# Hybrid diffusion step on one core: the norm modulation of two tiles on ScalarE and GpSimd, and layer 1 adaLN units taken at other places

## The reference, cut to what matters

```python
def _modulate(x, shift, scale):
    return _layernorm(x) * (1 + scale) + shift

for i in range(DEPTH):
    sh_a, sc_a, g_a, sh_f, sc_f, g_f = _ada(c, w_ada[i], b_ada[i])
    h = _modulate(x, sh_a, sc_a)
    out = attention(h) if i % 2 == 0 else _fourier_mix(h, w_fourier_out[0])
    x = _post_norm(x, g_a * out, ln_gain[i, 0], ln_bias[i, 0])
    h = _modulate(x, sh_f, sc_f)
    moe = _hier_moe(h, ...)
    x = _post_norm(x, g_f * moe, ln_gain[i, 1], ln_bias[i, 1])
```

## Time and profile before

| | us |
|---|---|
| median of 3 runs | 1063.76 (1063.31 to 1065.43) |
| profiled execution, own time | 1065.38 |
| its span, first to last instruction | 1063.6 |
| TensorE busy | 835.2 (79%) |
| VectorE busy | 329.9 (31%) |
| ScalarE busy | 166.0 (16%) |
| GpSimd busy | 158.7 (15%) |
| DMA | 318.11 MB, 299 GB/s mean |

### The profile page before, as it was taken

How to read it: one execution, slowest core, us unless ns; L and a number is a source line. 1 busy time by engine, 2 the same in 40 slices (tenths; PEclk the granted TensorE clock), 3 DMA queues, 4 the chain that set the end, 5 groups by cost and what they waited for, 6 DMA issues and landing times.

```text
span 1063.6 us, 13809 instructions
## 1 busy us (share of the span) xinstructions
PE 835.2 (79%) x4921; PEld 442.9 (42%) x4922; DVE 329.9 (31%) x803; ACT 166.0 (16%) x354; POOL 158.7 (15%) x245
## 2 busy tenths in 40 slices
PE   3899999969987888988778855997589877787740
PEld 3556565635466333323323334664533322332310
DVE  2113555544754111111111128247411110111117
ACT  0122222233010111111111112110111111101110
POOL 1032030311111120211101101101111111101010
...
GB/s 336 367 350 91 220 176 130 80 367 82 235 328 248 165 417 260 420 421 420 419 412 407 347 309 375 204 252 178 227 217 421 420 420 419 419 417 413 368 127 79
DMA packets 90242, 318.11 MB, mean 299 GB/s; under 512 B 13150, under 2 KB 26174, under 8 KB 65624
## 3 DMA queue, kind: packets, MB, share of 16 engines
...
## 4 chain that ended last, share of the span: by engine, by line
PE 50%; DMA 35%; DVE 6%; issue 4%; SPq 2%; ACT 2%; POOL 1%; ACTq 0%; DVEq 0%; POOLq 0%
DMA ring<-in_w_expert_up 24%; PE psum L916 15%; PE psum L799 8%; DMA ring<-in_w_ada 6%; PE psum L745 6%; PE psum L938 4%; PE psum L694 4%; PE psum L771 3%; DMA arena<-h_scratch,gidx 2%; DMA y_scratch<-arena,sidx 2%; PE psum L903 1%; DMA arena<-y_scratch 1%; SPq L366 1%; PE psum L1091 1%; PE psum L850 1%
## 5 line engine op out<-in xcount | busy, mean ns | idle before, releaser
L916 PE MATMUL psum<-ring,arena 128*64 128x512 f32 x1088 | 260.0, 633 | 60.6 <-DMA ring<-in_w_expert_up 56.6
L916 PEld LDWEIGHTS psum<-ring,arena 128*64 128x64 f32 x1088 | 93.4, 146 | 223.2 <-issue 221.1
L938 PE MATMUL psum<-ring,arena 128*64 128x512 f32 x544 | 125.9, 604 | 30.9 <-DVE arena L1666 29.6
L1662 DVE TENSOR_TENSOR arena<-arena,psum 128x256 f32<-128x256 f32 x34 | 14.3, 421 | 309.6 <-ACT arena L1215 309.6
L799 PE MATMUL psum<-ring,hT 128*128 128x384 f32 x288 | 98.2, 495 | 0.0
L938 PEld LDWEIGHTS psum<-ring,arena 128*64 128x64 f32 x544 | 40.2, 138 | 93.2 <-issue 77.8
L694 PE MATMUL psum<-ring,silu 128*32 128x128 f32 x1536 | 55.8, 305 | 27.4 <-DMA ring<-in_w_ada 26.9
L576 POOL DMA_INDIRECT y_scratch<-arena,sidx x34 | 34.4, 1012 | 250.9 <-DVE arena L1672 250.9
L745 PE MATMUL psum<-ring,hT 128*128 128x512 f32 x160 | 70.2, 595 | 1.1 <-ACT hT L1288 0.7
L799 PEld LDWEIGHTS psum<-ring,hT 128*128 128x128 f32 x288 | 54.5, 194 | 35.0 <-issue 1.5
L1672 DVE COPY arena<-psum 128x512 f32<-128x512 f32 x34 | 23.5, 692 | 134.4 <-PE psum L938 134.4
...
## 6 DMA issues: line engine op xcount, KB each, us to landing
...
```

Of the source, the lines that this page charges most:

```text
L916: last = pe.matmul(bank[b][64 * e:64 * e + 64, :].rearrange("p (g n) -> p g n", g=2), mem.GT[b][:, c, 64 * e:64 * e + 64], w, start=(c == ...
L938: last = pe.matmul(bank[5 + half][64 * e:64 * e + 64, :], mem.actT[b][:, f, 64 * e:64 * e + 64], w[:, f, 512 * half:512 * half + 512], sta ...
```

## The change

The modulation of tiles 0 and 1 leaves VectorE. VectorE makes statistics, the negated mean and variance; GpSimd makes the root and the product -mean * rstd (`normbias`); ScalarE makes x * rstd + normbias over 1024 columns; GpSimd multiplies by the scale row and adds the shift row, each in two halves of 512. Tile 2 stays on VectorE. Rows for prompt and sample have a buffer each; the sample's are loaded right after the gates in layer 0, and after the prompt's shift and the position matmuls in layer 1. Layer 1's unit 1 is made in attention stage 4 beside unit 0; unit 2 follows the prompt tile's turn, unit 3 the first two routers, units 4 and 5 the last router, and none is left behind the tables. The weight pieces alternate between regions, and expert 1 is loaded after unit 3, experts 2 and 3 after unit 5. In GpSimd's queue the first head root goes ahead of `store_m`. In stage 4 `project_head` goes ahead of the value product. The projections of both sample tiles run before any turn. Semaphore declarations and the wait of `head_transposes` for 13 units at head 7 are left out below.

```diff
@@ -50,16 +50,16 @@
-BETWEEN = {1: [(0, 4), (0, 5), (0, 6)], 2: [(0, 7), (0, 8), (0, 9)], 3: [(0, 10), (0, 11)], 4: [(1, 0)]}
-SPOTS = {3: (1, 3, 5), 2: (1, 4), 1: (4,)}
-PLACES = {"Q0": 0, "Q1": 24, "A0": 48, "A1": 64, "A2": 80, "B0": 0, "B1": 16, "B2": 32}
+BETWEEN = {1: [(0, 4), (0, 5), (0, 6)], 2: [(0, 7), (0, 8), (0, 9)], 3: [(0, 10), (0, 11)], 4: [(1, 0), (1, 1)]}
+SPOTS = {1: (1, 3, 5), 2: (1, 3, 5), 3: (1, 4), 4: (1, 4)}
+PLACES = {"Q0": 0, "Q1": 24, "A0": 48, "A1": 64, "A2": 80, "C1": 24, "B0": 0, "B1": 16, "B2": 32}
-PLACE.update({("ada", 1, u): "A2" for u in range(6)})
+PLACE.update({("ada", 1, u): place for u, place in enumerate(("A2", "C1", "A2", "C1", "A0", "A1"))})
...
@@ -140,6 +140,8 @@
         self.rstd = sb("rstd", [P, TILES])
+        self.negmean = sb("negmean", [P, TILES])
+        self.normbias = sb("normbias", [P, TILES])
         self.mx = sb("mx", [P, 2, 2])
@@ -214,7 +216,8 @@
         self.G = [view(0, D), view(4, D), view(46, D)]
-        self.lnshift = view(46, D)
+        self.lnscale = [self.lnscale_p[:, :], view(12, D)]
+        self.lnshift = [view(46, D), view(26, D)]
         self.wr_group = view(46, 2 * KC * GROUPS).rearrange("p (l n) -> p l n", l=2)
...
@@ -339,15 +344,22 @@
-                at = [(4, 0), (1, 1), (1, 2), (1, 3), (7, 0), (6, 0), (2, 0), (7, 0), (3, 0), (2, 0), (7, 0), (2, 0)][u]
+                at = [(4, 0), (4, 0), (1, 1), (1, 2), (1, 3), (7, 0), (2, 0), (7, 0), (3, 0), (2, 0), (7, 0), (2, 0)][u]
-        ADA_AFTER = {(0, 1): (0, 2), (0, 3): (0, 1), (1, 9): (1, 6), (1, 10): (1, 7), (1, 11): (1, 9)}
+        ADA_AFTER = {(0, 1): (0, 2), (0, 3): (0, 1), (1, 1): (1, 0), (1, 9): (1, 6), (1, 10): (1, 7), (1, 11): (1, 9)}
+
+        def wait_expert_row(eng, l, t):
+
+            if t < TILES - 1:
+                eng.wait_ge(mod_ready, 2 * l + t + 1)
+            else:
+                eng.wait_ge(last_ready, l + 1)
@@ -419,19 +431,21 @@
             load("ada", 1, 0)
-            for e in range(2):
-                sp.wait_ge(qkv_ps, 18 + 6 * e)
-                load_expert(0, e)
-            for u in range(1, 4):
-                after_ada(1, u - 1)
+            sp.wait_ge(qkv_ps, 18)
+            load_expert(0, 0)
+            sp.wait_ge(qkv_ps, 24)
+            load("ada", 1, 1)
+            for u in (2, 3):
+                after_ada(1, u - 2)
                 load("ada", 1, u)
             sp.wait_ge(proj_ps, 6)
-            load_expert(0, 2)
             for u in (4, 5):
-                after_ada(1, u - 1)
                 load("ada", 1, u)
+            after_ada(1, 3)
+            load_expert(0, 1)
             after_ada(1, 5)
-            load_expert(0, 3)
+            for e in (2, 3):
+                load_expert(0, e)
             for l in range(2):
@@ -594,33 +608,61 @@
 
+            HALVES = [slice(0, 512), slice(512, D)]
+
+            def scale(l, t):
+
+                i, n = (0 if t == 0 else 1), 2 * l + t + 1
+                pool.wait_ge(root_out, roots[0])
+                pool.tensor_tensor(mem.normbias[:, t:t + 1], mem.negmean[:, t:t + 1], mem.rstd[:, t:t + 1], ALU.mult
+                                   ).then_inc(bias_out, 1)
+                pool.wait_ge(rows_in_for[i], 32 * (l + 1))
+                pool.wait_ge(centred, n)
+                for part in HALVES:
+                    last = pool.tensor_tensor(mem.tmp[:, t, part], mem.tmp[:, t, part], mem.lnscale[i][:, part], ALU.mult)
+                link(last)
+
+            def shift(l, t):
+
+                i = 0 if t == 0 else 1
+                for part in HALVES:
+                    last = pool.tensor_tensor(mem.h[:, t, part], mem.tmp[:, t, part], mem.lnshift[i][:, part], ALU.add)
+                last.then_inc(mod_ready, 1)
+
             def norm_rows(l, i):
-                spread(mem.lnscale[:, :], l, 4, i, lnscale_in)
-                spread(mem.lnshift, l, 3, i, lnshift_in)
-
+                spread(mem.lnscale[i], l, 4, i, rows_in_for[i])
+                spread(mem.lnshift[i], l, 3, i, rows_in_for[i])
+
+            head_root()
             store_m(0, 4, ADA_UNITS, ADA_AT[0, 11])
             pool.wait_ge(router_ready, 4)
             norm_rows(0, 0)
-            for _ in range(3):
+            for _ in range(2):
                 head_root()
...
                 spread(mem.gates[:, i, :], 0, 2, i, gates_in[i])
+            norm_rows(0, 1)
 
...
                 if l == 1:
-                    pool.wait_ge(norm_ready, 9)
+                    pool.wait_ge(norm_ready, 6)
                     spread(mem.gates[:, 1, :], 1, 2, 1, gates_in[1])
...
                 for t in range(TILES):
-                    for _ in range(2):
-                        root([t])
-                    if t == 0:
-                        pool.wait_ge(norm_ready, 6 * l + 4)
-                        norm_rows(l, 1)
+                    root([t])
+                    if t >= 1 + l:
+                        shift(l, t - 1)
+                    root([t])
+                    if t < TILES - 1:
+                        scale(l, t)
+                    if t == 0 and l == 1:
+                        shift(l, t)
+                        pool.wait_ge(four_ps, KC + 2)
+                        norm_rows(1, 1)
                 if l == 1:
@@ -674,7 +716,7 @@
                     if l == 0 and tiles == [0]:
-                        pool.wait_ge(norm_ready, 7)
+                        pool.wait_ge(norm_ready, 4)
                         spread(mem.gates[:, 0, :], 1, 2, 0, gates_in[0])
...
@@ -864,7 +906,7 @@
             for u in range(1, 5):
-                spots = SPOTS[len(BETWEEN[u])]
+                spots = SPOTS[u]
                 for s in range(6):
@@ -878,12 +920,12 @@
                         ada(*BETWEEN[u][spots.index(s)])
+                    if u == 4 and s >= 1:
+                        project_head(s - 1)
                     if g >= 1:
...
                         turn_head(s)
-                        if s >= 1:
-                            project_head(s - 1)
             pd_transposes(STEPS - 1)
@@ -974,34 +1016,30 @@
 
-                project(l, 1, (2, 3), (0,))
-                if l == 0:
-                    pe.wait_ge(proj_used, 2)
-                    ada(1, 1)
-                project(l, 1, (2, 3), (1,))
-                project(l, 2, (6, 7), (0,))
-                pe.wait_ge(norm_ready, 6 * l + 4)
+                project(l, 1, (2, 3))
+                project(l, 2, (6, 7))
+                wait_expert_row(pe, l, 0)
+                pe.wait_ge(proj_used, 6 * l + 2)
                 turn(0, (4, 5), strided=True)
                 if l == 0:
                     ada(1, 2)
-                project(l, 2, (6, 7), (1,))
-                if l == 0:
-                    ada(1, 3)
-                pe.wait_ge(norm_ready, 6 * l + 5)
+                wait_expert_row(pe, l, 1)
                 wait_turn(pe, TURN_ROUTE[l], 0)
...
                     pe.wait_ge(router_ready, 4)
-                pe.wait_ge(proj_used, 6 * l + 2)
                 router(l, 0)
                 wait_turn(pe, TURN_ROUTE[l], 1)
                 router(l, 1)
-                pe.wait_ge(norm_ready, 6 * l + 6)
+                if l == 0:
+                    ada(1, 3)
+                wait_expert_row(pe, l, 2)
                 turn(2, (4, 5), strided=True)
...
                     ada(1, 4)
+                    ada(1, 5)
                     pe.wait_ge(tables_in, 16)
@@ -1025,8 +1063,6 @@
                     last.then_inc(table_ps, 1)
-                if l == 0:
-                    ada(1, 5)
 
@@ -1036,7 +1072,7 @@
             def turn_tile(t):
-                pe.wait_ge(norm_ready, 7 + t)
+                pe.wait_ge(norm_ready, 4 + t)
                 turn(t, TURN_BANKS[t])
@@ -1225,7 +1261,11 @@
                 for t in range(TILES):
-                    act.wait_ge(norm_ready, 6 * l + 4 + t)
+                    if t < TILES - 1:
+                        act.wait_ge(bias_out, 2 * l + t + 1)
+                        nc.scalar.activation(mem.tmp[:, t, :], mem.x[:, t, :], ACT.Identity, bias=mem.normbias[:, t:t + 1],
+                                             scale=mem.rstd[:, t:t + 1]).then_inc(centred, 1)
+                    wait_expert_row(act, l, t)
                     act.dma_start(h_dram[l].rearrange("(k t p) n -> t p k n", k=2, p=P)[t],
@@ -1544,14 +1584,19 @@
                         dve.wait_ge(gb_used, 2 * l + 1)
+                    if t < TILES - 1:
+                        link(tile_stats(t))
+                        link(V.bn_aggr(mem.mv[:, t, :], mem.stats[:, t, :, :].rearrange("p i n -> p (i n)")))
+                        V.tensor_scalar(mem.negmean[:, t:t + 1], mean, -1.0, None, ALU.mult)
+                        roots[0] += 1
+                        V.tensor_scalar(mem.rs_v[:, t:t + 1], mem.mv[:, t, 1:2], EPS, None, ALU.add).then_inc(spread_in, 1)
+                        continue
                     finish_stats(tile_stats(t), [t])
-                    dve.wait_ge(lnscale_in, 16 * (2 * l + 1 + i))
```

(11 more changed lines are left out.)

20 lines of the change are left out of this document (11 added, 9 removed).

## The result

The changed kernel takes 1069.45 us (median of 8 runs, 1066.64 to 1070.58), the kernel before, run beside it, 1063.37 us (8 runs, 1060.45 to 1065.43): ratio 1.006, 95% interval 1.0044 to 1.0076. It is slower, by about 6 us where 10 were forecast. The profiled execution took 1070.1 us with a span of 1068.3, 4.7 above the span before.

The account below looks back on a forecast made before the run. TensorE bounds half the span, weights in flight most of the rest, so the expert loops' starts decide. Layer 0 (3.2) and layer 1 (7.2) sum to 10.4, taken as 10 us later: 1073.8 us, range 1058.5 to 1078.

Parts of the forecast that it names:

- the sum: Whole kernel: layer 0 3.2 us later plus layer 1 7.2 us later, 10.4, taken as 10 us.
- Attention: Attention up to the first projection: early root ends VectorE's waits, 7.3 us sooner, bounds 4.8 and 7.5.
- Both waits that the sum names: VectorE in attention: 4.8 us of the root wait go, and 2.49 us for transposes, through moved unit and earlier output projection.
- Layer 0 up to the position matmuls: Layer 0, projections to routing: row at 307.5, router 4.2 us later, position matmuls 2.0 us later.
- Last turn 1.5 and router 2.7, both between their two levels: Layer 0, last tile on TensorE: times set between full and half clock, since a unit ahead may bring the clock back.
- Gather: Layer 0's first gather: lands in 9.2 us beside experts 2 and 3, 4.6 us more, between 0 and 6.
- Cold first pair: Layer 0's first expert pair: half clock, 10.09 us against 7.09, and 0.9 in the turn, 3.9 us more.
- Layer 0 in all: Layer 0 including attention: 2.0 + 4.6 + 3.9 - 7.3, 3.2 us later.
- Layer 1: Layer 1, projections to last router: same order without units, ends at 758.7 instead of 751.5, 7.2 us later.
- The clock rival: Turns and routers in both layers: TensorE stays at full clock, sum -2.9, 1060.9 us; chance 0.2.
- The rival in which ScalarE's queue does not hold the centring: Sample's first tile: row 2.5 us earlier in each layer, and gather lands in 4.57; 1064.6 us, chance 0.15.
- The rival without the attention gain: Attention: head 6's root waits for the store instead, so no gain; 1079 to 1081 us, chance 0.1.

Follow-up runs that it names:

- root_first: The kernel before with one edit: GpSimd takes one head root ahead of the store of m; 1053.79 us, ratio 0.993.
- late_experts: The changed kernel with expert 3's load held until TensorE has turned the first gathered pair; 1065.0 us, ratio 1.0023.
- best: The changed kernel with VectorE modulating all tiles, expert 3's load held for the first gathered pair, sample's rows spread after tile 0's first root; 1053.89 us, ratio 0.9917.
- best2: As best, but the loads of experts 2 and 3 both held until TensorE has turned the first gathered pair; 1051.78 us, ratio 0.9899.
- warm: The changed kernel with 48 (layer 0) and 60 (layer 1) unused transposes in TensorE's hole ahead of the sample's first turn; 1062.05 us, ratio 1.0001.
- act_first: The changed kernel with ScalarE's centring of tile 1 ahead of its eviction of the turned tile 0; 1065.86 us, ratio 1.003.
- after_mended: The changed kernel plus act_first, router_early, sample's rows spread after the first root, and experts 2 and 3 held for the first gathered pair; 1053.99 us, ratio 0.9917.
- dve_mod: The changed kernel with the modulation of tiles 0 and 1 given back to VectorE, the other moves kept; 1056.19 us, ratio 0.9941.
- router_early: The changed kernel with tile 0's routing product ahead of the wait for tile 1's row; 1062.59 us, ratio 0.9996.

## Why the prediction was right, and where it was off

Direction, place and mechanism were those forecast, and 1069.45 us lies within the range of 1058.5 to 1078. The size was 10 forecast against 6 measured (4.7 between the two profiled spans). Stage by stage against the sum, from the timelines:

- **Attention, -7.3 forecast, -8.2 measured**, beyond the bound of 7.5. The store's landing did not touch head 6's root (root at 242.83, well behind the spreads at 235.03). Both waits that the sum names fell: the one for the root by 4.7 us, the one of 2.49 us to 0.22. In no term stands the last output projection ahead of the long run. It took 1.98 us in the changed kernel (TensorE's timeline above, granted clock 1.00), and in the kernel before, at a granted clock of 0.53:

```profile
266.36 3.68 PE L860 MATMUL psum<-ring,hT 128*128 128x512 f32 x4 [0.57 <-ACT hT L1103]
```

root_first tells the parts apart. The root alone gives 7.2 us from the cache store to S0, and with it the wait of 2.49 us is gone too (0.24 there), while its last output projection is still at 3.64 us. The forecast put that wait down to the moved unit and the earlier output projection. It goes with the root. What the changed kernel gains beyond that, 1.1 us, comes with its other moves in attention.

- **Layer 0 up to the position matmuls, +2.0 forecast, +0.1 measured.** Tile 1's row came at 306.9 in the old time, forecast 307.5. The last turn began at 319.1, forecast 320.3 (the row 0.6, the products 6.88 for 7.2, overlaps). The term "Last turn 1.5 and router 2.7, both between their two levels" came out at 1.18 and 2.12, close to full clock behind the unit. So the router ended 2.1 us later than before and not 4.2. The positions ran at full clock too (1.55 us at 320.82), and the tables were done 1.2 us sooner behind them; that saving was in no term.
- **Gather, +4.6 forecast, +4.6 measured.** From the end of the table's matmuls to the first gathered rows TensorE had 4.3 us before (337.85 to 342.17) and waited 8.9 now. The gather was issued at 328.24 and its rows were there at 337.43: 9.2 us, as taken, with 421 to 424 GB/s moving beside it. The cause is shown twice: the wait followed the weights in flight in late_experts (5.03) and in best and best2 (8.28 to 4.18).
- **Cold first pair, +3.9 forecast, +3.1 measured:** 9.43 against 7.09, and 0.8 in the turn.
- **Layer 0 in all: +3.2 forecast, -1.6 measured** (0.1 - 1.2 + 4.6 + 3.1 - 8.2). Of the 5.7 us between the sum of 10.4 and the 4.7 measured, 4.8 are here, 0.9 of them in attention. The first loop then lost 1.2 us (S1-G0, 355.3 against 354.1) that I had taken as fixed. In it, around 646 to 658 us, a run of channel matmuls took 6.74 us instead of 5.32 and a unit 3.24 instead of 1.95; the kernels without the moved units show 354.1 and 354.2, those with them 354.6 to 355.3. Why is open.
- **Layer 1, +7.2 forecast, +6.0 measured.** The row came at 37.2 us behind S1, forecast 37.5; the two products took 6.88 and not 7.2, and the turns in front of them overlapped a little. The first pair, taken as unchanged, was 1.0 us shorter, within what it varies by without an edit.

Sum measured, with 0.1 for what lies between these stages and behind them: -1.6 + 1.2 + 6.0 - 1.0 + 0.1 = 4.7. The errors partly cancel: layer 0 came out 4.8 us and layer 1 2.2 us better than forecast, the loop 1.2 us worse.

**The rivals.** The clock rival was priced at 1060.9 us, with a sum of -2.9 where the forecast has 10.4, 13.3 us apart. Its condition was absent, with holes of 6.66 and 8.54 us. warm, which makes a part of it by force, took 1062.05 us, but that nearness is luck in part: its step from the changed kernel is 0.59%, some 6.3 us, its last turn in layer 1 is at half clock again, and against the kernel before it is level and not 2.9 us ahead. The rival in which ScalarE's queue does not hold the centring promised 2.5 us in each layer; act_first gave 0.4 and 2.6. In layer 0 GpSimd's small product was done at 290.0, 0.8 us before ScalarE centred; in layer 1 at 728.3, 6.1 us before. That rival had taken both layers alike. The rival without the attention gain is out, for the gain was there.

**What the forecast did not ask.** It priced the work handed over and never what VectorE would do with the time it gets back. after_mended and dve_mod show the answer for layer 1: it waits for TensorE. There the relief was worth nothing from the start, not only outweighed. Of the 1.2% that the hand-over costs, about 0.6% is the half clock in the hole that it opens (warm), and these overlap with the queue orders (act_first 0.3%, router_early 0.64%). The single gains add up to more than the whole, as they would if each shortened the same path between hole and last router.
